# RWKV bonus sums formed once a head and spread later, and the sample values' products put ahead of the turned key tiles, in a one-layer HGRN2 + RWKV-7 + mixture-of-experts step

## Chip, cores, metric

One core of a Trainium2 chip. The metric is the device time of one execution in microseconds. TensorE is called PE here, VectorE DVE, ScalarE ACT, GpSimd POOL; SP is the engine that issues most of the DMAs.

## What is computed (the reference, cut)

A prompt of 256 rows and 64 sample rows (8 sequences of 8 tokens) of width 1024 go through one layer. After a norm and one input projection, half of the columns feed an HGRN2 group (4 heads of 128) and half an RWKV-7 group (8 heads of 64); their outputs are joined, projected and added; then comes a top-4-of-32 mixture of experts. The change touches only the RWKV group:

```python
k = k * (1.0 + (a - 1.0) * k_a)
S = S * w_t + sa * (kk_t * a_t) + v_t * k_t      # per token; y_t = S r_t
y = group_norm(y) * lnx_w + lnx_b
bonus = jnp.sum(r_h * k_h * r_k, axis=-1, keepdims=True) * v_h     # one sum a head and token
y = (y + bonus) * g
```

The experts' weights are 32 x (8 + 4) MiB, read once.

## The kernel before, in words

Everything is float32 and kept with features on the 128 partitions: an array such as `rbon`, `rr`, `rk`, `rv` holds four tiles j, each of 128 features (two heads of 64) by 320 tokens. The engines run one hand-written stream each, tied by semaphores. PE's stream sets the order of the first 300 us; its results go to eight PSUM banks by a table, `psum_units`: each unit (a stage with a number) is given a bank, `free(stage, i)` makes PE wait until the unit that held the bank before has been read (`<stage>_ready`), and `filled` counts `unit_filled` up, on which the readers wait (`wait_filled`).

In the order of PE's stream, around the change: `kss` and `kspread` (L1008, L1027; a sum over each head by 32 columns of the block matrix `blk`, and its spreading by a column of the identity, for the key norms), the HGRN outputs `ho` and `hosa` (up to L1086), the HGRN state product `hs2` (L1014) and projection 23, then the RWKV products `gM`, `gN`, `gT` (L1126, L1136), and a long solve. Behind it come:

- `Ys` (L1318 to L1320): the sample rows' values. For each j and each head p of the tile, three products of 64x64 add up in one quarter of bank 0. After each j stand four transposes of 128x128 (L1313), which turn a key tile (`btok`, `ktok`) to tokens.
- `UW` and `UX` (L1332), in two token tiles, then `bonus` (L1339): per j one product of the full `blk` with `rbon`, which gives each head's sum already on all of its 64 rows, in banks 4, 5, 0, 1.
- `C` (L1351), `S0` (L1505, L1508, in banks 3 and 4), `sendl`/`sendh` (L1490), `Q` (L1520), `Y0` (L1537, L1540).

ACT reads `btok`, `ktok`, `Ys`, `UW` and one `UX` out of PSUM (L2158 to L2165), DVE the other `UX` (L2775, L2776), with the decay of the sample states (`decayed`, L2771) before and after it, and then multiplies the four bonus banks by `rv` into `rbon` (L2781). POOL sends out the sample states of HGRN in eight DMAs (L837).

SP waits at L640 for these eight to have landed (`hgrn_out`) and for `Y0`, then reloads the input rows and begins the stream of the experts' weights, in pieces of 2 and then 4 MiB, into slots that it gets back from PE (`w_used`):

```python
sync.wait_ge(S("hgrn_out"), 16 * (NS + 1))
sync.wait_ge(S("unit_filled"), U("Y0", 2))
```

Of the kernel before, what the change touches and what calls it, by code (L numbers as in the profile page):

```python
# [81 lines left out]
def psum_units():  # L82

    u, turn, ends = [], [0], []

    def add(stage, n=1, at=None, ended=True):
        k = sum(1 for s, _, _ in u if s == stage)
        for i in range(n):
            if at is None:
                u.append((stage, k + i, turn[0] % 8))  # L90
                turn[0] += 1
            else:
                u.append((stage, k + i, at[i]))
            if ended:
                ends.append((stage, k + i))

    def end(stage, k):
        ends.append((stage, k))
    add("nmT", 1, (0,))
    add("hT", KT, (1, 2, 3, 4, 5, 6, 7, 0))  # L100
    add("proj", 1, (1,), ended=False)
    add("bc", 1, (2,))
    add("params", 1, (3,))
    end("proj", 0)
    turn[0] = 3
    add("proj", 12)
    turn[0] += 3
    for i, h in enumerate(LEVELS):
        if i % 2:
            add("proj", 2)  # L110
        if h < 64:
            add("lvl")
        else:
            add("cross")
        if h <= 4:
            add("seq")
    add("lvl")
    add("seq")
    add("proj")
    add("kstok", 3)  # L120
    for j in range(4):
        for stage, o in (("wpre", 0), ("apre", 4)):
            add(stage, 1, ((turn[0] + o + j) % 8,))
    add("gpre", 4)
    add("proj")
    t = turn[0]
    add("kss", 1, (t % 8,))
    add("hs1", 1, ((t + 4) % 8,))
    add("proj", 1, ((t + 5) % 8,), ended=False)
    add("kspread", 4, tuple((t + i) % 8 for i in range(4)))  # L130
    end("proj", 21)
    turn[0] = t + 6
    add("ho", 2)
    add("hosa", ended=False)
    add("proj")
    end("hosa", 0)
    add("hs2", 1, (1,))
    add("proj", 1, (7,))
    add("gM", 3, (2, 3, 1))
    add("gN", 3, (4, 5, 6))  # L140
    add("gT", 2, (7, 0))
    add("s0t", 4, (5, 6, 7, 0))
    add("gT", 1, (1,))
    add("Z", 3, (2, 3, 4))
    add("proj", 1, (5,))
    add("W", 3, (6, 7, 0))
    add("T", 3, (1, 2, 3))
    add("proj", 1, (4,), ended=False)
    add("Z", 3, (5, 6, 7))
    end("proj", 25)  # L150
    add("W", 3, (0, 1, 2))
    add("T", 3, (3, 4, 5))
    add("gK", 3, (6, 7, 0))
    add("proj", 1, (1,), ended=False)
    add("Z", 2, (2, 3))
    add("gRb", 3, (4, 5, 6))
    end("proj", 26)
    add("W", 2, (7, 0))
    add("T", 2, (1, 2))
    add("ht", 3, (4, 5, 6))  # L160
    add("proj", 1, (3,))
    add("vtok", 3, (4, 5, 6))
    add("Z", 2, (7, 0))
    add("Rs", 2, (1, 2), ended=False)
    add("proj", 1, (3,))
    add("W", 2, (4, 5))
    add("T", 2, (6, 7))
    end("Rs", 0)
    end("Rs", 1)
    add("hsend", 4, (0, 3, 4, 5))  # L170
    add("proj", 1, (6,))
    add("Z", 2, (4, 5))
    add("Us", 1, (1,))
    add("gRk", 3, (2, 3, 4))
    add("atok", 2, (5, 6))
    add("R0", 2, (7, 0))
    add("bks", 1, (1,))
    add("hsend", 4, (2, 3, 4, 5))
    add("W", 2, (6, 7))
    add("Ys", 1, (0,), ended=False)  # L180
    add("btok", 2, (1, 2))
    add("ktok", 2, (3, 4), ended=False)
    end("ktok", 0)
    end("Ys", 0)
    end("ktok", 1)
    for x in range(2):
        add("UW", 1, (6 + x,))
        add("UX", 1, (2 + x,))
    add("bonus", 4, (4, 5, 0, 1))
    add("C", 2, (6, 7))  # L190
    add("S0", 2, (3, 4), ended=False)
    add("sendl", 1, (2,))
    add("sendh", 1, (5,))
    end("S0", 0)
    end("S0", 1)
    add("Q", 2, (0, 1))
    add("sendl", 1, (2,))
    add("sendh", 1, (5,))
    add("Y0", 2, (6, 7))
    add("yc", 1, (2,))  # L200
    u.append(("xo", 1, 0))
    add("var", 1, (5,))
    add("yc", 1, (1,))
    u.append(("xo", 2, 3))
    add("var", 1, (4,))
    add("yc", 1, (6,))
    add("pst", 1, (5,))
    u.append(("xo", 0, 7))
    end("xo", 0)
    add("var", 1, (5,))  # L210
    end("xo", 1)
    end("xo", 2)
    add("h2T", 1, (4,))
    u.append(("xo", 3, 2))
    add("logit", 1, (5,))
    add("h2T", 2, (1, 6))
    u.append(("xo", 4, 7))
    add("fold", 1, (4,))
    add("logit", 1, (3,))
    add("fold", 1, (5,))  # L220
    end("xo", 3)
    add("h2T", 1, (1,))
    add("rank", 1, (0,))
    end("xo", 4)
    add("h2T", 1, (2,))
    add("logit", 1, (3,))
    add("fold", 1, (0,))
    add("rank", 1, (3,))
    add("bias", 1, (2,))
    assert len(ends) == len(u)  # L230
    return u, ends
# [82 lines left out]
def build(nc, A, O):  # L314
    ctx = ExitStack()
    with ctx:
# [539 lines left out]
        def _(pe):  # L856
            mm = nc.tensor.matmul

            def free(stage, i):

                n_ = UPOS[stage, i]
                if BEFORE[n_] is not None:
                    s, k, _ = UNITS[BEFORE[n_]]
                    s, k = {"nmT": ("params", 1), "bc": ("params", 2), "params": ("params", 3), "hT": (("hT", "hTo_lb")[k % 2], k // 2), "S0": ("S", k + 2), "Y0": ("Y", k), "xo": ("xo", k + 1)}.get(s, (s, k))
                    pe.wait_ge(S(f"{s}_ready"), k + 1)
                return banks[BANK[n_]]

# [215 lines left out]
            for y in range(2):  # L1083
                for p in range(2):
                    r = slice(64 * p, 64 * p + 64)
                    last = mm(b[r, P * y:P * y + P], ats[r, y, :], itoks[r, y, :], start=False, stop=True, skip_group_check=True)  # L1086
            filled(last, "hosa")
            hstate("hs2", 1)
            proj(23, 24)

# [18 lines left out]
            def half(x):  # L1109

                return slice(64 * x, 64 * x + 64)
# [202 lines left out]
                filled(last_, stage)  # L1314
            for j in range(4):
                for p in range(2):
                    o = b[half(p), half(j)]
                    mm(o, us[half(p), j, :], Rb_[2][half(p), j, :], start=True, stop=False, skip_group_check=True)  # L1318
                    mm(o, vtoks[half(p), j, :], Rk_[2][half(p), j, :], start=False, stop=False, skip_group_check=True)
                    last = mm(o, yts[half(p), j, :], ident[half(p), half(p)], start=False, stop=True, skip_group_check=True)  # L1320
                if j == 3:
                    filled(last, "Ys")
                turn_tokens(("btok", "ktok")[j // 2], (ra, rk)[j // 2], j % 2)
            pe.wait_ge(S("W_ready"), upto(4))
            pe.wait_ge(S("R0_ready"), 2)
# [1 line left out]
            for tile in range(2):  # L1327
                b = [free("UW", tile), free("UX", tile)]
                for j in range(4):
                    for a in range(2):  # L1330
                        for p in range(2):
                            last = mm(b[p][half(a ^ p), P * j:P * j + P], W_[p][half(a), 4 * tile + j, :], RA[half(a), p, tile, j, :],  # L1332
                                      start=True, stop=True)
                            if (j, a) == (3, 1):
                                filled(last, ("UW", "UX")[p])
            pe.wait_ge(S("rbon_in"), 4)
            for j in range(4):
                b = free("bonus", j)
                filled(mm(b[:, 0:NT], blk[:, :], rbon[:, j, :], start=True, stop=True), "bonus")  # L1339

            def head(x_, p_):
                return slice(P * (x_ % 4) + 64 * p_, P * (x_ % 4) + 64 * p_ + 64)
# [632 lines left out]
        def _(act):  # L1975
# [56 lines left out]
            for n, (j, _, _) in enumerate(PROJ):  # L2032
# [51 lines left out]
                if n == 21:  # L2084

                    act.wait_ge(S("cen_ready"), 1)
                    a(ec[:, :, :], cen[:, :, :], ACT.Exp, scale=-EDEC)
                    act.wait_ge(S("cen_ready"), 2)
                    act.wait_ge(S("unit_filled"), U("kss", 1))
                    a(tB[:, :, :], tA[:, :, :], ACT.Exp, scale=EDEC).then_inc(S("exp_ready"), 1)  # L2090
                    a(rs[:, :, :], rs[:, :, :], ACT.Exp, scale=-EDEC).then_inc(S("exp_ready"), 1)
                    act.wait_ge(S("exp_ready"), 1)
                    a(tA[:, :, :], tA[:, :, :], ACT.Exp, scale=-EDEC).then_inc(S("exp_ready"), 1)
                    for tile in range(2):
                        ready(cp(htok[:, 512 * tile:512 * tile + 512], wait_filled("ho", tile)[:, :]), "ho")
                    ready(cp(htok[:, 1024:W5], wait_filled("hosa", 0)[:, 0:256]), "hosa")
                    act.wait_ge(S("ho_ready"), 2)
                    act.wait_ge(S("hosa_ready"), 1)
                    act.wait_ge(S("ks_row_scale"), 1)
                    a(hsq, htok, ACT.Square).then_inc(S("osq"), 1)  # L2100
                if n == 23:
                    act.wait_ge(S("ks_row_scale"), 1)
                    for x in range(3):
# [295 lines left out]
        def _(dve):  # L2399
# [376 lines left out]
            signal(v.tensor_copy(o[64:128], b[0:64, :]), "UX_ready")  # L2776
            decayed(1)
            dve.wait_ge(S("gpre_ready"), 4)
            for j in range(4):
                b = wait_filled("bonus", j)  # L2780
                signal(v.tensor_tensor(rbon[:, j, :], rv[:, j, :], b[:, 0:NT], ALU.mult), "bonus_ready")  # L2781
# [141 lines left out]
            sent(0)  # L2923
            step_state(0)
            sent(1)
            dve.wait_ge(S("bonus_ready"), 4)
            for j in range(4):
                signal(v.scalar_tensor_tensor(out=rbon[:, j, :], in0=rbon[:, j, :], scalar=pcol("lnb", j), in1=rg[:, j, :],
                                              op0=ALU.add, op1=ALU.mult), "bg_ready")
# [226 lines left out]
```

## Time and profile before

| | |
|---|---|
| median of 3 runs | 1212.01 us (1211.21 to 1215.73) |
| the profiled execution | 1214.35 us, of which the span of the trace is 1212.4 us |
| PE busy | 1187.4 us (98%) |
| DVE, ACT, POOL busy | 440.9, 259.5, 44.7 us |
| read from HBM | 430.01 MB |
| granted PE clock | 0.998 of full speed over the span |

The profile is one execution. A row of the timeline has the start in us, the time from the first start to the last end, the engine, line, operation, operands and count, and in brackets the idle time ahead of it and what ended that. PE records each float32 matmul as two, so x8 are four matmuls; matmul rows overlap their neighbours, so what a group costs is read from start to start.

### The profile page before, as it was taken

What the parts mean: (1) busy time and instruction counts of PE and PEld (TensorE: products, weight loads), DVE (VectorE), ACT (ScalarE), POOL (GpSimd) and SP (SyncE); (2) the same over time, 40 slices, a digit from 0 to 9 for tenths busy, and PEclk for the clock granted to TensorE, in tenths of its full rate; (3) what the DMA queues carried; (4) which work ended last, traced back from release to release, by engine and by line L of the source; (5) the groups of instructions that cost most, each with busy time, mean ns of one, the idle gap of its engine ahead of it and who ended that gap; (6) DMA issues with size and microseconds to landing.
All of it is one profiled execution on the core that took longest, in us unless ns stands there. A gap on an engine that the chain in (4) does not pass through costs nothing.

```text
span 1212.4 us, 18239 instructions
## 1 busy us (share of the span) xinstructions
PE 1187.4 (98%) x7814; PEld 572.9 (47%) x7814; DVE 440.9 (36%) x962; ACT 259.5 (21%) x630; POOL 44.7 (4%) x101
## 2 busy tenths in 40 slices
PE   8999999999999999999999999999999999999996
PEld 6777677745344344444443444344444444343332
DVE  3357954753413332332233132313322323232324
ACT  3114435422221111111121212021111111111213
POOL 8000110100000000000000000000000000000000
PEclk9999999999999999999999999999999999999999
DMA  9732302498999999999999999999999999999996
GB/s 285 183 105 71 122 31 72 125 414 334 409 426 429 426 414 428 426 432 431 431 429 431 431 431 432 431 426 431 429 432 432 430 430 431 432 432 428 422 424 231
DMA packets 49387, 436.09 MB, mean 360 GB/s; under 512 B 11525, under 2 KB 26952, under 8 KB 31770
## 3 DMA queue, kind: packets, MB, share of 16 engines
q1 hardware_dynamic: 48180, 431.74, 86.4%
q0 software_dynamic: 960, 3.02, 0.8%
q8 instruction: 63, 1.03, 0.3%
q10 hardware_dynamic: 166, 0.15, 0.0%
q14 instruction: 18, 0.15, 0.0%
HBM read 430.01 MB, written 4.89 MB: 359 GB/s over the span
## 4 chain that ended last, share of the span: by engine, by line
PE 86%; DMA 10%; DVE 2%; issue 1%; SPq 0%; ACT 0%; DVEq 0%
PE bank L1634 33%; PE bank L1670 16%; PE bank L914 9%; PE bank L1600 7%; DMA ring<-in_w_gate_up 5%; PE bank L1704 4%; PE bank L1395 3%; DMA ring<-in_w_down 3%; PE bank L1661 3%; DMA mix<-in_w_gate_up 2%; PE bank L1695 1%; PE bank L1152 1%; PE bank L901 1%; PE bank L947 1%; DMA hx<-in_state_shift 0%
## 5 line engine op out<-in xcount | busy, mean ns | idle before, releaser
L1634 PE MATMUL bank<-ring,mix 128*64 128x512 f32 x1504 | 344.8, 598 | 3.3 <-DMA ring<-in_w_gate_up 3.1
L1634 PEld LDWEIGHTS bank<-ring,mix 128*64 128x64 f32 x1504 | 101.3, 136 | 201.0 <-issue 197.7
L1670 PE MATMUL bank<-ring,mix 128*64 128x512 f32 x736 | 168.2, 598 | 0.8 <-DMA ring<-in_w_down 0.8
L2986 DVE TENSOR_TENSOR hTb<-bank,w2a 128x512 f32<-128x512 f32 x32 | 22.1, 692 | 361.3 <-PE bank L1661 361.3
L914 PE MATMUL bank<-hTb,ring 128*128 128x328 f32 (+1 forms) x416 | 120.6, 444 | 0.0
L2218 ACT ACTIVATE mix<-bank,nf 128x256 f32<-128x256 f32 x64 | 26.8, 470 | 431.3 <-PE bank L1600 431.2
L1634 PE MATMUL bank<-mix 128*64 128x512 f32 x500 | 112.7, 595 | 1.8 <-DMA mix<-in_w_gate_up 1.8
L3046 DVE TENSOR_TENSOR mix<-mix,bank 128x512 f32<-128x512 f32 x70 | 48.2, 688 | 159.5 <-PE bank L1704 143.5
L914 PEld LDWEIGHTS bank<-hTb,ring 128*128 128x128 f32 x416 | 77.8, 192 | 33.8 <-issue 2.0
L1670 PEld LDWEIGHTS bank<-ring,mix 128*64 128x64 f32 x736 | 49.3, 136 | 89.9 <-issue 84.0
L1634 PEld LDWEIGHTS bank<-mix 128*64 128x64 f32 x500 | 35.1, 137 | 71.7 <-issue 70.0
L1600 PE MATMUL bank<-mix,hx 128*128 128x256 f32 x240 | 66.1, 418 | 0.0
L3014 DVE SCALAR_TENSOR_TENSOR y_low<-bank,gc,y_high 64x512 fp32r<-64x512 f32 x62 | 46.5, 750 | 49.6 <-ACT y_high L2293 49.1
L1600 PEld LDWEIGHTS bank<-mix,hx 128*128 128x128 f32 x240 | 55.5, 300 | 9.1 <-issue 8.4
L2293 ACT ACTIVATE y_high<-bank,gc 64x512 fp32r<-64x512 f32 x62 | 42.3, 682 | 74.1 <-DVE gc L3028 38.3
L2273 ACT COPY g2w<-bank 128x512 f32<-128x512 f32 x64 | 34.3, 593 | 99.8 <-PE bank L1634 99.8
L1670 PE MATMUL bank<-mix 128*64 128x512 f32 x240 | 54.8, 598 | 0.0
L1704 PEld LDWEIGHTS bank<-y_high,slot_rows 128*128 128x128 f32 (+1 forms) x96 | 16.2, 186 | 62.5 <-issue 62.5
L1661 PEld LDWEIGHTS bank<-idg,g2w 128*128 128x128 f32 x256 | 33.2, 209 | 26.0 <-issue 26.0
L2283 ACT ACTIVATE bank<-hTb 128x512 f32<-128x512 f32 x32 | 19.2, 602 | 113.9 <-DVE hTb L2988 113.9
L1704 PE MATMUL bank<-y_high,slot_rows 128*128 128x512 f32 (+1 forms) x96 | 42.3, 480 | 0.0
L1661 PE MATMUL bank<-idg,g2w 128*128 128x128 f32 x256 | 39.3, 296 | 0.0
(448 smaller groups left out, 1086.7 us busy)
## 6 DMA issues: line engine op xcount, KB each, us to landing
ring<-in_w_gate_up SPq DMA_DIRECT2D x30, 4096.0 KB, 22.9
ring<-in_w_gate_up SPq DMA_DIRECT2D x33, 2048.0 KB, 14.4
ring<-in_w_down SPq DMA_DIRECT2D x15, 4096.0 KB, 23.7
mix<-in_w_gate_up SPq DMA_DIRECT2D x10, 4096.0 KB, 23.7
ring<-in_w_down SPq DMA_DIRECT2D x14, 2048.0 KB, 13.8
mix<-in_w_gate_up SPq DMA_DIRECT2D x11, 2048.0 KB, 13.2
mix<-in_w_down SPq DMA_DIRECT2D x5, 4096.0 KB, 25.0
ring<-in_w_in SPq DMA_DIRECT2D x14, 1024.0 KB, 5.5
```

Source lines behind the costliest of these rows:

```text
L914: last_ = mm(b_[:, 0:nn], slot(chunk)[:, c, P * k:P * k + P], hT[:, c, 0:nn], start=(c == 0), stop=(c == KT - 1))
L1395: last_ = mm(o_, lhs_, wo[c_ // 4][:, c_ % 4, 512 * h_:512 * h_ + 512], start=(c_ == 0), stop=(c_ == KT - 1))
L1600: last_ = mm(o, rows_of(tile_, c, r), sel[tile_][0:TN[tile_], :], start=(first and tile_ == TORD[0]), stop=(tile_ == TORD[2]), skip_group_ ...
L1634: last_ = mm(b_[64 * half:64 * half + 64, :].rearrange("s (p q) -> s p q", q=4), toks, cols[:, half], start=(c == 0), stop=(c == KT - 1))
L1661: last_ = nc.tensor.transpose(b_[:, P * q:P * q + P], src[:, q:NCOL:4], ident[:, :])
L1670: last_ = mm(b_[r:r + 64, :], lhs, w[:, o:o + NCOL], start=(j == 0 and q == 0), stop=(j == 1 and q == 3))
L1704: last_ = mm(o[:, :], scatr[r[g], g, P * tile_:P * tile_ + P], y_[r[g], g, :], start=(y_ is yhir and g == half), stop=(stop and y_ is ylor ...
L2218: ins = a(xg[n // 4 % 2][:, 256 * c:256 * c + 256], b[:, 256 * x:256 * x + 256], ACT.Copy, scale=nf2[int(n // 4 >= EW // 4)][:, c:c + 1])
L2273: cp(o, b[:, :]).then_inc(S("gu_read"), 1)
L2293: ins = a(yhir[r, k, :], banks[2][r, :], ACT.Copy, scale=gc[r, g:g + 1])
L3014: ins = v.scalar_tensor_tensor(out=ylor[r, k, :], in0=banks[2][r, :], scalar=gc[r, g:g + 1], in1=yhif[r, k, :], op0=ALU.mult, op1=ALU.subt ...
L3046: ins = v.tensor_tensor(o, o, b[:, :], ALU.add)
```

## The change

A new unit `bsum` stands after `hosa`, in bank 0: four matmuls sum `rbon` over each head, every tile j into 32 rows of one bank, with every fourth column of `blk`. ACT copies that bank into `rbon[:, 0, :]`, after its square of the HGRN rows. Late in the stream `bonus` no longer multiplies with `blk`: per j, two matmuls that contract over 32 rows spread one row each over the 64 rows of a head. DVE now waits for all four bonus units before it overwrites `rbon`. And all of `Ys` runs first, with the two heads p side by side, before the 16 transposes.

```diff
@@ psum_units
     end("hosa", 0)
+    add("bsum", 1, (0,))
     add("hs2", 1, (1,))
...
-    add("Ys", 1, (0,), ended=False)
+    add("Ys", 1, (0,))
     add("btok", 2, (1, 2))
-    add("ktok", 2, (3, 4), ended=False)
-    end("ktok", 0)
-    end("Ys", 0)
-    end("ktok", 1)
+    add("ktok", 2, (3, 4))
@@ PE
             filled(last, "hosa")
+            pe.wait_ge(S("rbon_in"), 4)
+            b = free("bsum", 0)
+            for j in range(4):
+                last = mm(b[32 * j:32 * j + 32, 0:NT], blk[:, 0:P:4], rbon[:, j, :], start=True, stop=True)
+            filled(last, "bsum")
             hstate("hs2", 1)
@@ PE
             for j in range(4):
                 for p in range(2):
-                    o = b[half(p), half(j)]
-                    mm(o, us[half(p), j, :], Rb_[2][half(p), j, :], start=True, stop=False, skip_group_check=True)
-                    mm(o, vtoks[half(p), j, :], Rk_[2][half(p), j, :], start=False, stop=False, skip_group_check=True)
-                    last = mm(o, yts[half(p), j, :], ident[half(p), half(p)], start=False, stop=True, skip_group_check=True)
-                if j == 3:
-                    filled(last, "Ys")
+                    mm(b[half(p), half(j)], us[half(p), j, :], Rb_[2][half(p), j, :], start=True, stop=False, skip_group_check=True)
+                for p in range(2):
+                    mm(b[half(p), half(j)], vtoks[half(p), j, :], Rk_[2][half(p), j, :], start=False, stop=False, skip_group_check=True)
+                for p in range(2):
+                    last = mm(b[half(p), half(j)], yts[half(p), j, :], ident[half(p), half(p)], start=False, stop=True,
+                              skip_group_check=True)
+            filled(last, "Ys")
+            for j in range(4):
                 turn_tokens(("btok", "ktok")[j // 2], (ra, rk)[j // 2], j % 2)
@@ PE
-            pe.wait_ge(S("rbon_in"), 4)
+            pe.wait_ge(S("bonus_ready"), 1)
             for j in range(4):
+                r = slice(32 * j, 32 * j + 32)
                 b = free("bonus", j)
-                filled(mm(b[:, 0:NT], blk[:, :], rbon[:, j, :], start=True, stop=True), "bonus")
+                for p in range(2):
+                    c = 32 * j + 16 * p
+                    last = mm(b[half(p), 0:NT], ident[r, c:c + 1].broadcast_to([32, 64]), rbon[r, 0, :], start=True, stop=True)
+                filled(last, "bonus")
@@ ACT
                     a(hsq, htok, ACT.Square).then_inc(S("osq"), 1)
+                    ready(cp(rbon[:, 0, :], wait_filled("bsum", 0)[:, 0:NT]), "bonus")
@@ DVE
             dve.wait_ge(S("gpre_ready"), 4)
+            dve.wait_ge(S("unit_filled"), U("bonus", 4))
             for j in range(4):
                 b = wait_filled("bonus", j)
                 signal(v.tensor_tensor(rbon[:, j, :], rv[:, j, :], b[:, 0:NT], ALU.mult), "bonus_ready")
```

Line numbers after the change are some 2 to 11 higher than before. PE's stream between the last rows of the solve (L1152 before, L1155 after) and the transposes, before:

```order
L1152 MATMUL bank<-mix,hx 64x32 x31
L1318 MATMUL bank<-ring 64x64 [waits Us_ready,R0_ready,gRk_ready,gRb_ready]
L1319 MATMUL bank<-ring 64x64
L1320 MATMUL bank<-idg,lor 64x64
L1318 MATMUL bank<-ring 64x64
L1319 MATMUL bank<-ring 64x64
L1320 MATMUL bank<-idg,lor 64x64
L1313 MATMUL bank<-idg,mix 128x128 [waits bks_ready]
L1313 MATMUL bank<-idg,mix 128x128 x3
```

and the same place after, where L1320, L1322 and L1324 are the three products of `Ys` and L1316 the transposes:

```order
L1155 MATMUL bank<-mix,hx 64x32 x31
L1320 MATMUL bank<-ring 64x64 [waits Us_ready,R0_ready,gRk_ready,gRb_ready]
L1320 MATMUL bank<-ring 64x64
L1322 MATMUL bank<-ring 64x64 x2
L1324 MATMUL bank<-idg,lor 64x64 x2
L1320 MATMUL bank<-ring 64x64 x2
L1322 MATMUL bank<-ring 64x64 x2
L1324 MATMUL bank<-idg,lor 64x64 x2
```

The group of six stood four times with four transposes behind each; now the four groups follow each other, each product for both heads at once, and the 16 transposes come after them. The second place is PE's stream from `bonus` to the first products of `S0`, before:

```order
L1339 MATMUL bank<-mix,g2w 128x320 [waits ktok_ready,rbon_in]
L1339 MATMUL bank<-mix,g2w 128x320 [waits hsend_ready]
L1339 MATMUL bank<-mix,g2w 128x320 [waits Ys_ready]
L1339 MATMUL bank<-mix,g2w 128x320 [waits btok_ready]
L1351 MATMUL bank<-hTb,ring 64x64 [waits UX_ready,UW_ready,ktok_ready,btok_ready]
L1351 MATMUL bank<-hTb,ring 64x64 x31
L1505 MATMUL bank<-ring,hTb 64x64 [waits bonus_ready,UX_ready]
```

and after, where L1347 is `bonus`, L1360 `C` and L1514 the first product of `S0`:

```order
L1347 MATMUL bank<-mix,idg 64x320 [waits ktok_ready,bonus_ready]
L1347 MATMUL bank<-mix,idg 64x320
L1347 MATMUL bank<-mix,idg 64x320 [waits hsend_ready]
L1347 MATMUL bank<-mix,idg 64x320
L1347 MATMUL bank<-mix,idg 64x320 [waits Ys_ready]
L1347 MATMUL bank<-mix,idg 64x320
L1360 MATMUL bank<-hTb,ring 64x64 [waits UX_ready,UW_ready,ktok_ready,btok_ready]
L1360 MATMUL bank<-hTb,ring 64x64 x31
L1514 MATMUL bank<-ring,hTb 64x64 [waits bonus_ready,UX_ready]
```

Eight narrow matmuls stand for the four full ones, and the waits of what follows are the same.

## Rows read from the trace of the kernel before

**Rows 1.** Windows, whole kernel: stretch, length, busy of each engine, PEclk, DMA share, GB/s
```profile
600.00:800.00 200.00, 200.00 (x875) 83.43 (x876) 60.05 (x138) 33.06 (x86) 0.00 (x0) 1.00 1.00 430
```
**Rows 2.** Waits of SP's queue: who waited for whom, total, times, longest
```profile
SPq L640 <- PE bank L1540: 47.4, 1, 47.4
```
**Rows 3.** Timeline of SP's queue, start of the weight stream
```profile
236.57 0.49 SPq L587 DMA_DIRECT2D hx<-in_x_sample  x1
...
238.21 2.33 SPq L587 DMA_DIRECT2D ring<-in_w_gate_up  x5
```
**Rows 4.** Timeline of PE, 118 to 146 us, around the new unit's place
```profile
119.85 0.77 PE L1008 MATMUL bank<-hx,g2w 128*32 128x320 f32 x8
...
125.51 0.79 PE L1027 MATMUL bank<-mix,idg 32*64 32x320 f32 x16
...
136.82 0.65 PE L1086 MATMUL bank<-ring 64*64 64x128 f32 x8
...
142.91 1.16 PE L1126 MATMUL bank<-mix 64*64 64x64 f32 x64
145.75 0.62 PE L1136 MATMUL bank<-mix 64*64 64x64 f32 x13 [1.68 <-DVE ring L2624]
```
**Rows 5.** Timeline of ACT, same stretch
```profile
137.97 1.27 ACT L2100 ACTIVATE ring<-mix 128x1280 f32<-128x1280 f32 x1
139.15 0.41 ACT L2056 COPY raw<-bank 128x328 f32<-128x328 f32 x1
```
**Rows 6.** Timeline of DVE, same stretch
```profile
131.52 1.94 DVE L2603 SCALAR_TENSOR_TENSOR mix<-mix,par 128x320 f32<-128x320 f32 x4
...
140.97 0.48 DVE L2479 TENSOR_TENSOR hx<-raw 128x319 f32<-128x319 f32 x1
```
**Rows 7.** Chain that ended last, 207 to 226 us: start, us, what
```profile
207.96 0.41 PE bank L1283 x13
...
216.00 0.22 PE bank L1318 x2
...
216.63 0.59 PE bank L1313 x4
...
220.95 1.91 PE bank L1332 x64
222.86 2.35 PE bank L1339 x8
225.21 1.09 PE bank L1351 x64
```
**Rows 8.** Timeline of PE, 226 to 232 us
```profile
226.12 0.30 PE L1505 MATMUL bank<-ring,hTb 64*64 64x64 f32 x8
...
231.43 1.96 PE L1490 MATMUL bank<-ring,lor 32*64 32x256 f32 x32 [0.21 <-issue]
```
**Rows 9.** Timeline of ACT, 220 to 225 us
```profile
220.99 0.59 ACT L2158 COPY hTb<-bank 128x512 f32<-128x512 f32 x1 [0.66 <-PE bank L1313]
...
224.11 0.58 ACT L2165 COPY ring<-bank 64x512 f32<-64x512 f32 x1
```
**Rows 10.** Timeline of DVE, 220 to 241 us
```profile
220.47 1.28 DVE L2771 TENSOR_TENSOR mix<-mix,pc 128x512 f32<-128x512 f32 x2
222.15 0.69 DVE L2775 COPY ring<-bank 64x512 f32<-64x512 f32 x1 [0.40 <-PE bank L1332]
...
224.90 1.68 DVE L2781 TENSOR_TENSOR mix<-mix,bank 128x320 f32<-128x320 f32 x4
...
240.74 0.42 DVE L2791 TENSOR_TENSOR mix<-bank,dc 128x256 f32<-128x256 f32 x1 [4.58 <-PE bank L1364]
```
**Rows 11.** Line L837, POOL's eight DMAs: durations in ns, first and last start
```profile
L837 POOL DMA_DIRECT2D out<-ring x8: 750/751/763, 217.1 to 228.9; - x8
...
DMA to landing us min/median/max: 3.0/3.4/4.2
```
**Rows 12.** Waits of PE, 118 to 300 us: total, times, longest
```profile
PE bank L1152 <- issue: 1.8, 2, 1.4
```

More of the change, by code:

```diff
@@ L863, in free @@
                     s, k, _ = UNITS[BEFORE[n_]]
-                    s, k = {"nmT": ("params", 1), "bc": ("params", 2), "params": ("params", 3), "hT": (("hT", "hTo_lb")[k % 2], k // 2), "S0": ("S", k + 2), "Y0": ("Y", k), "xo": ("xo", k + 1)}.get(s, (s, k))
+                    s, k = {"nmT": ("params", 1), "bc": ("params", 2), "params": ("params", 3), "hT": (("hT", "hTo_lb")[k % 2], k // 2), "S0": ("S", k + 2), "Y0": ("Y", k), "xo": ("xo", k + 1), "bonus": ("bonus", k + 1), "bsum": ("bonus", 0)}.get(s, (s, k))
                     pe.wait_ge(S(f"{s}_ready"), k + 1)
@@ L2925, in _ @@
             sent(1)
-            dve.wait_ge(S("bonus_ready"), 4)
+            dve.wait_ge(S("bonus_ready"), 5)
             for j in range(4):
```

## The prediction

> **What bounds the kernel now.** I read the windows first. In the experts' part [rows 1] the DMA engines are busy all the time (share 1.00, 430 GB/s) while PE's records overlap without a gap. The weights are 32 x 12 MiB, 402.7 MB, and at 430 GB/s they take about 936 us of the 1212; nothing in the change touches that part. So the end of the kernel is the start of the weight stream, plus bytes over rate, plus what the slots hold it up on the way. The second view is SP's queue: it sat 47.4 us in one wait at L640, released by L1540, the last product of `Y0` [rows 2]; the input rows are issued at 236.57 and the first weights at 238.21 us [rows 3]. The wait before it, for POOL's eight DMAs, had ended by then: the last was issued at 228.9 us, is 0.75 us long and lands in 3.0 to 4.2 us [rows 11], so at 232.7 to 233.9 us, some 2.7 to 3.9 us before SP moved. What the change is worth is therefore how much earlier `Y0` is filled, one for one, up to 2.7 us and a little beyond. After `Y0` everything (output projection, router, first slots) hangs on the same chain and moves with it.
>
> **The early place: bsum.** It adds four matmuls of 128 rows by 32 columns over 320 tokens. That is the very shape of `kss`, whose eight records take 0.77 us [rows 4]. They stand behind `hosa`, which starts at 136.82 us and takes 0.65, so at about 137.5 us. Their input was ready at 131.52 + 1.94 = 133.46 us [rows 6]: no wait. All behind it on PE's queue (`hs2`, projection 23, `gM`) moves by 0.77: `gM` from 142.91 to 143.68. But the third part of `gM` waits 1.68 us for DVE's L2624 at 145.75 us [rows 4]. The cover is 1.68 us, the cost 0.77, so nothing is left to pay, as long as DVE is not made later itself. DVE would be, if ACT were late: ACT gets one more copy of 128x320 (0.41 us, the nearest copy) between the square that starts at 137.97 and the `raw` copy at 139.15 [rows 5]. `bsum` is full at about 138.3, before the square ends, so ACT does not wait; the raw copy ends at 139.56 + 0.41 = 139.97, and DVE reads it at 140.97 [rows 6]. 1.0 us of slack is left. If both covers were gone, this part would cost 0.77 or up to 1.2 us; the bound below nothing is excluded, since nothing is removed here. I take 0.
>
> **The late place on PE alone.** From the start of `Ys` to `UW` now: 220.95 - 216.00 = 4.95 us. It is four times 12 records of 64x64 in 216.63 - 216.00 = 0.63 us (52 ns each) and four transposes in 0.59 us [rows 7]. After it the products run as pairs of heads. The nearest row is L1283, 13 records in 0.41 us, 32 ns each: the same two quarters of the array, the same one bank [rows 7]. 48 x 0.032 = 1.54, and 4 x 0.59 = 2.36 for the transposes (an upper bound, they now follow each other): 3.90, so 1.05 us less. `bonus` is now 2.35 us [rows 7]; its new form is that of `kspread`, 16 records in 0.79 us [rows 4]: 1.56 less. Together PE could be 2.6 us earlier at `C`, at 225.21 - 2.6 = 222.6 us.
>
> A rule speaks against the first of these. The Trainium skill, TensorEngine Tiling (Array Packing), Restrictions and Gotchas (Gotcha 1: PSUM Pressure), says that different row tiles cannot access the same PSUM bank at once. By it the heads' pairs would not overlap in bank 0, and `Ys` would stay at 52 ns a record. By this rule, the row of L1283 does not agree, since its two row halves write one bank at 32 ns a record.
>
> **What C waits for then.** `C` needs both `UX` and both `UW`. With PE alone, the second `UX` is full at 216.00 + 3.90 + 1.91 = 221.8 us. ACT then has three copies of 0.58 us with 0.02 between (`UW` and the two halves of `UX`, the last of which now starts at 224.11) [rows 9], so it is done at 223.6. It comes that far in time: of the key copies the last, which now starts at 220.99 behind a wait for L1313 [rows 9], starts about 1 us earlier too. DVE copies the first `UX`: it waits only 0.40 us for it now, behind a `decayed` of 1.28 us that starts at 220.47 and is not held by PE [rows 10]. So DVE gains 0.40 us and no more: copies at 221.75 instead of 222.15, done at 223.1. `C` starts at 223.6 (now 225.21) and ends, 1.09 later [rows 7], at 224.7.
>
> **What S0 waits for: the term that decides.** `S0` takes bank 4, which held bonus unit 0, so PE waits until DVE has multiplied that unit into `rbon`. Now DVE's four multiplications start at 224.90 and take 1.68 us [rows 10]; the first is done at about 225.38 (0.48 us for a first 128x320 on DVE, as the row of L2479 [rows 6]), and PE comes at 226.12 [rows 8], 0.74 us later: hidden. After the change DVE starts 0.40 earlier, at 224.50 (the new wait for all four bonus units ended at about 222.6 on PE), and unit 0 is free at 224.98. PE has been ready since 224.7, and starts `S0` at 225.02. That is 226.12 - 225.02 = 1.10 us earlier. PE then comes out of an idle instead of a full pipeline; today the first record of `S0`, at 226.12, overlaps the end of `C` at 225.21 + 1.09 = 226.30 [rows 7, 8] by 0.18, and that overlap is lost in part. I take off 0.1. Gain: 1.0 us of the 2.6.
>
> Behind it nothing takes more. `sendh` and `Q` need bonus units 1 to 3, freed at 0.40 us steps. The 0.21 us idle at 231.43 [rows 8] is, I think, DVE's sum out of the first `send` products, which follows PE and moves with it. Further on DVE waits 4.58 us for PE at 240.74 [rows 10], so it has room.
>
> **Sum.** 0 (early place) - 1.0 (late place) = -1.0 us. Against the profiled execution: 1214.35 - 1.0 = 1213.35, span 1211.4. That execution lies 2.3 us above the median of the runs, so the forecast for the median is 1212.01 - 1.0 = 1211.0 us.
>
> **Rivals.**
> - *All of PE's gain arrives* (-2.6 us, 1209.4): if DVE's work before the bonus is shorter than I read. For it: PE's saving is solid. Against: DVE's stretch from 220.47 to 226.6 has one gap, of 0.40 us [rows 10]. 0.10.
> - *The pairs in one bank do not overlap.* `Ys` stays at 4 x 0.63 + 2.36 = 4.9 us; only `bonus` gains. The second `UX` is full at 222.8, ACT done at 224.7, `C` ends at 225.8, 0.46 us earlier than now, and `S0` with it: -0.5 us with a little less idle, 1211.5. For it: the single records of L1318. Against: L1283. This is what the skill's page would make of it. 0.10.
> - *Nothing arrives* (1212.0): the gain is eaten between `Y0` and the slots, where the stream waits for several steps of the router. 0.20.
> - *Slower.* PE stands still for up to 1.4 us at places where nothing is waited for (L1152, issue 1.8 us in two stops [rows 12]). The change puts 8 records more ahead of the solve and 8 more into `bonus`. If that brings one more such stop, or makes one longer, in the stretch from 147 to 216 us where PE never waits for another engine, it is paid in full: +1.4 - 1.0 = +0.4, 1212.4, and with a second, 1213.8. It decides from 1.0 us of added standstill on. For it: the stops are there. Against: few records are added. 0.15.
> - *The forecast*, -0.7 to -1.3: 0.45.
>
> **Range and chances.** The cases reach from 1209.4 to 1213.8. A median of a few runs moves by itself: three runs before lay between 1211.21 and 1215.73. Leaving out the outer tenths I say 1208.9 to 1213.8; the likeliest case alone 1210.4 to 1211.9. No change under 0.5% (6 us) can be told by a measurement of this kernel from none, and all cases lie within 3 us: within 0.5% 0.95, faster 0.02, slower 0.03 (a bound on the weight stream that I do not see).
>
> **What would show it.** Right: `kss`'s 0.77 us again at the new line before `hs2`, and PE's wait for L2624 cut from 1.68 to about 1.0; `Ys` and the transposes in 3.9 us or a little less; `bonus` in 0.8; PE idle for about 1 us before `C`, released by ACT's last `UX` copy, and 0.3 us before `S0`, released by DVE's first multiplication; first weights at about 237.2 us. Wrong: no idle before `S0` (then DVE was earlier), 12 records of `Ys` in 0.6 us (no overlap), SP released by POOL's DMAs instead of PE, or an end that does not follow the start of the weights.

## The result and the profile after

| | before | after |
|---|---|---|
| median of runs, us | 1212.49 (22 runs, 1210.91 to 1215.73) | 1215.73 (22 runs, 1212.91 to 1217.45) |
| ratio to before | | 1.0024, 95% interval 1.0018 to 1.0031 |
| profiled execution, time / span, us | 1214.35 / 1212.4 | 1214.93 / 1213.2 |
| instructions | 18239 | 18274 |
| PE records | | 7830, busy 1185.3 us |

The change costs 0.24%, about 2.9 us (the two medians, which the ratio does not go by, lie 3.2 apart), where a gain of 1.0 us was forecast. The time lies above the range. The loss is under the 0.5% taken as the bound of what can be told, but 22 runs a side tell it from nothing.

The weight stream is as before [rows 1], by the windows of the same stretch (all engines, PEclk, DMA share, GB/s):

```profile
600.00:800.00 200.00, 200.00 (x877) 83.59 (x877) 59.74 (x138) 33.05 (x86) 0.00 (x0) 1.00 1.00 430
```

The start of the stream is still PE's to decide, and it did not come earlier by 1 us net. These rows of after are from the waits and the timeline of SP's queue, and answer to [rows 2, 3]; the last one is the first group of transfers in the stream proper:

```profile
SPq L638 <- PE bank L1549: 46.4, 1, 46.4
...
236.07 0.49 SPq L585 DMA_DIRECT2D hx<-in_x_sample  x1
...
237.71 2.37 SPq L585 DMA_DIRECT2D ring<-in_w_gate_up  x5
...
297.30 7.57 SPq L585 DMA_DIRECT2D ring<-in_w_gate_up  x4
```

That last group starts at 297.01 us in the trace of before. From it to the end of the span are 1212.4 - 297.01 = 915.4 us before and 1213.2 - 297.30 = 915.9 after, and between 914.6 and 915.9 in every kernel below. So what is won or lost lies ahead of it.

**The two places that the change edits** went as forecast in this trace. PE's timeline of after (start, us, what, idle before and its releaser), to be held against [rows 4, 7, 8]:

```profile
135.65 0.77 PE L1089 MATMUL bank<-mix,g2w 128*32 128x320 f32 x8
...
144.00 0.62 PE L1139 MATMUL bank<-mix 64*64 64x64 f32 x13 [0.98 <-DVE ring L2634]
...
216.33 0.33 PE L1320 MATMUL bank<-ring 64*64 64x64 f32 x4
216.46 0.31 PE L1322 MATMUL bank<-ring 64*64 64x64 f32 x4
216.58 0.31 PE L1324 MATMUL bank<-idg,lor 64*64 64x64 f32 x4
...
217.87 1.96 PE L1316 MATMUL bank<-idg,mix 128*128 128x128 f32 x16
219.79 1.98 PE L1337 MATMUL bank<-ring,hx 64*64 64x128 f32 x64
221.69 0.79 PE L1347 MATMUL bank<-mix,idg 32*64 32x320 f32 x16
223.95 1.16 PE L1360 MATMUL bank<-hTb,ring 64*64 64x64 f32 x64 [1.46 <-ACT ring L2175]
225.53 0.34 PE L1514 MATMUL bank<-ring,hTb 64*64 64x64 f32 x8 [0.42 <-DVE mix L2792]
```

`bsum` takes 0.77 us and the wait for DVE behind it fell from 1.68 to 0.98. `Ys` and its transposes take 219.79 - 216.33 = 3.46 us in place of 4.95, `bonus` 0.79 in place of 2.35. PE then waits where it was forecast to wait, for ACT's last `UX` copy and for DVE's first bonus multiplication, whose rows in the timelines of ACT and DVE are:

```profile
223.01 0.58 ACT L2175 COPY ring<-bank 64x512 f32<-64x512 f32 x1
```
```profile
222.14 0.69 DVE L2785 COPY ring<-bank 64x512 f32<-64x512 f32 x1
...
224.89 1.68 DVE L2792 TENSOR_TENSOR mix<-mix,bank 128x320 f32<-128x320 f32 x4
```

From the first record of `Ys` to the first of `S0` are 225.53 - 216.33 = 9.20 us. Before, the first single record of `Ys` stood at 215.93, and `S0` at 226.12: 10.19. The gain of the late place is 0.99 us in this trace, and it was a good one for it: the stretch is 10.2 us in all four traces of kernels with neither part, but 9.82 in a second trace of this same program (experiment 4) and 9.48 and 9.59 in the two variants of it in experiments 7 and 9. In the second trace DVE's first `decayed`, which does not hang on PE, stands 5.11 us behind the start of `Ys` and not 4.49, and `S0` is as much later. So the gain is 0.4 to 1.0 us, by how DVE stands; with the `Ys` part alone it is 0.3 to 0.5 (9.88 and 9.68), with the bonus part alone 0.1 (10.08, twice).

**Where the time went**: the stops of PE for which the profile names nothing ("issue"), ahead of both `Ys` and the stream. PE's timeline of after, these stops alone (one of 0.29 us at 230.89, of another kind, is left out):

```profile
151.27 1.66 PE L1155 MATMUL bank<-hx,mix 64*64 64x64 f32 x64 [1.46 <-issue]
...
162.83 0.30 PE L1163 MATMUL bank<-hx,mix 64*64 64x32 f32 x2 [0.85 <-issue]
...
172.74 0.31 PE L1163 MATMUL bank<-hx,mix 64*64 64x32 f32 x5 [0.49 <-issue]
...
201.34 0.46 PE L1275 MATMUL bank<-ring 64*32 64x64 f32 x32 [1.32 <-issue]
...
216.05 0.43 PE L1155 MATMUL bank<-mix,hx 64*64 64x32 f32 x14 [0.48 <-issue]
...
233.79 0.28 PE L1549 MATMUL bank<-ring 64*64 64x64 f32 x3 [0.35 <-issue]
...
237.53 0.50 PE L1385 MATMUL bank<-mix 64*64 64x64 f32 x9 [0.53 <-issue]
```

and of before (likewise without one of 0.21 us at 231.43):

```profile
153.10 0.99 PE L1152 MATMUL bank<-hx,mix 64*64 64x64 f32 x53 [1.40 <-issue]
...
172.39 1.09 PE L1126 MATMUL bank<-mix 64*64 64x64 f32 x59 [0.85 <-issue]
...
200.90 0.42 PE L1272 MATMUL bank<-ring 64*32 64x64 f32 x23 [1.12 <-issue]
...
215.69 0.31 PE L1152 MATMUL bank<-mix,hx 64*64 64x32 f32 x5 [0.37 <-issue]
...
234.53 0.28 PE L1540 MATMUL bank<-ring 64*64 64x64 f32 x3 [0.30 <-issue]
```

Before had no stop near 162 and none after `Y0` (the last of its rows lies in `Y0`). A stop can fall inside a group of equal records and cut it: in before, 8 of a group's 64 records stand ahead of the stop near 150 and 56 behind it, the 53 of the row and 3 more; in after all 64 stand behind. The stop comes 8 records earlier in the code, as many as `bsum` added. Between the first four stops of before its windows count PE's records (length, PE busy, records, PEclk, DMA share, GB/s):

```profile
151.75:171.60 19.85, 18.43 (x507) 1.00 0.10 40
171.60:199.85 28.25, 27.39 (x760) 1.00 0.22 78
199.85:215.40 15.55, 14.33 (x378) 1.00 0.01 3
```

507, 760 and 378 are about 4, 6 and 3 times 126.6: the stops stand at a fixed distance in the program, not where some work is done. Each record has a weight load beside it and there are some waits for semaphores between them, so 126.6 records are about 256 instructions. Counted with these, before's five stops fall on PE's instructions 2497, 3521, 5058, 5826 and 6850, those of after on 2498, 3010, 3521, 5057, 5825, 6849 and 7106. All of them are 193 or 194 above a multiple of 256. So is every "issue" stop of 0.30 us or more from 147 to 241 us in the fourteen traces, but for one at 195; the short ones (0.15 to 0.29 us) at L1490 or its counterpart are not, and are of another kind. The Trainium skill, Runtime: NRT & Kernel Launch, Instruction fetch mechanics, says that an engine's code comes in blocks of 256 instructions, and that crossing into one is mostly hidden. The distance agrees. "Mostly hidden" agrees by count and not by price: of the 20 such places from 147 to 241 us before shows a stop at five, and these cost 0.30 to 1.40 us. That what PE stops for is its code is thus a reading of these distances; no view shows the fetch itself.

Why the stop near 162 is new can be read off the same count. Instruction 3009 of before lies among the wide matmuls of a projection (128x328, eight records in 2.47 us from 162.08 on), and nothing stops there. With 16 instructions more ahead it lies two records (the x2 in the row of after) before that projection, among products of 64x32.

In the trace of after the stop near 150 is followed by a stretch at a granted clock of 0.50, the 1.2 GHz level. PE's windows of after, then of the change's bonus part alone (below), which had a longer stop and kept its clock:

```profile
150.00:152.00 2.00, 0.73 (x40) 0.93 1.03 418
152.00:154.00 2.00, 2.00 (x53) 0.50 0.33 125
154.00:156.00 2.00, 2.00 (x6) 0.72 0.01 2
```
```profile
152.00:154.00 2.00, 0.09 (x4) 1.00 1.01 410
154.00:156.00 2.00, 2.00 (x82) 1.00 0.24 88
```

The same two in PE's timeline, at the stop's end and at the next group of that line:

```profile
151.27 1.66 PE L1155 MATMUL bank<-hx,mix 64*64 64x64 f32 x64 [1.46 <-issue]
...
159.00 1.14 PE L1155 MATMUL bank<-mix,hx 64*64 64x32 f32 x64
```
```profile
153.91 1.16 PE L1158 MATMUL bank<-hx,mix 64*64 64x64 f32 x64 [2.28 <-issue]
...
160.07 1.14 PE L1158 MATMUL bank<-mix,hx 64*64 64x32 f32 x64
```

**One sum over the traces.** Each from one execution, us: from the release of `gM`'s third part (the row with the wait for L2634, or its counterpart) to SP's input rows; PE's "issue" stops in that stretch; from the input rows to the stream's group above; and the stop behind `Y0`, which lies there. Kernels that the next section introduces are in the table too.

| kernel | to input rows | stops in it | on to the stream | stop behind `Y0` |
|---|---|---|---|---|
| before (1214.35) | 90.8 | 4.25 | 60.4 | none |
| before, again (1212.43) | 89.0 | 3.08 | 60.4 | none |
| `Ys` part alone (1210.35) | 89.0 | 3.28 | 60.4 | none |
| bonus part alone (1214.39) | 90.9 | 5.04 | 60.6 | none |
| before + 4 idle matmuls (1215.30) | 90.6 | 4.23 | 61.2 | 0.66 |
| after (1214.93) | 92.1 | 5.24, and half clock | 61.2 | 0.53 |
| after, again (1215.94) | 92.2 | 5.40, and half clock | 61.8 | 1.08 |

The first trace of before is of an execution 1.9 us above its median, with stops to match; the second (experiment 3), at 1212.43, is the typical one. Against it after has 2.2 us more of stops up to the input rows, about 1.6 us for the half clock (for the same records 159.00 - 151.27 = 7.73 us against 160.07 - 153.91 = 6.16 in the bonus part alone, at full clock), and 1.0 less for the late place: +2.8 of the +3.1 us in the table. The stop behind `Y0` adds 0.8. That is 3.9 us in a pair of traces whose times differ by 2.5: the third part of `gM` is released at 145.76 in before and at 144.00 in after, with nothing edited that would make it earlier by that much. The repeat of after closes too: 2.3 of stops, 1.2 of half clock and 0.4 less for the late place are 3.1 of its +3.2. The idle matmuls' trace does not: the stops are 1.15 of its +1.68.

**The new stops over all traces.** Stops, us, at the two places that before does not have:

| kernels | near 162 | behind `Y0` |
|---|---|---|
| without added instructions (before twice, `Ys` part, and experiments 6, 8 and 11) | none in six traces | none in six |
| 16 more ahead of the solve (after twice, bonus part, idle matmuls, and experiments 7, 10 and 12) | 0.30 to 1.00 in all seven | 0.53 to 1.08 in six of seven |
| 256 more (experiment 9) | none | 0.77 |

### The profile page after: what moved, and what is told of

Same layout as the page of the kernel before. It is cut to its first block, busy times and chain, and to the rows that moved or that the text cites. A ratio compares the mean times of both kernels' runs of the same rounds, so it can differ in the third digit from the quotient of the medians.

```text
span 1213.2 us, 18274 instructions
## 1 busy us (share of the span) xinstructions
PE 1185.3 (98%) x7830; PEld 571.9 (47%) x7830; DVE 441.0 (36%) x962; ACT 259.6 (21%) x631; POOL 43.8 (4%) x101
## 4 chain that ended last, share of the span: by engine, by line
PE 86%; DMA 10%; DVE 3%; issue 1%; ACT 0%; SPq 0%; DVEq 0%
PE bank L1643 33%; PE bank L1679 16%; PE bank L912 9%; PE bank L1609 7%; DMA ring<-in_w_gate_up 5%; PE bank L1713 4%; PE bank L1404 3%; DMA ring<-in_w_down 3%; PE bank L1670 3%; DMA mix<-in_w_gate_up 2%; PE bank L1704 1%; PE bank L899 1%; PE bank L1155 1%; PE bank L945 1%; PE bank L1746 0%
```

## Experiments

Every ratio is to the kernel before on the same chip, with its 95% interval; in brackets this median and that of before, us. Theory A: the 8 records of `bsum` shift PE's later code against the places where PE stops for code. B: the new order of `Ys` costs. C: the waits and copies that `bsum` brings cost. D: the stop near 150 us is PE's next code queued behind the 2 MiB load of `w_out`.

**1 and 2. The change in two halves.** One kernel takes the order of `Ys` alone, one takes `bsum` and `bonus` alone.

```diff
 # ys_only
-    add("Ys", 1, (0,), ended=False)
+    add("Ys", 1, (0,))
...
 # bonus_only
+    add("bsum", 1, (0,))
...
```

> Before, with only the new order of Ys and the transposes. Theory A (the place of PE's instructions in the blocks in which its code comes decides how long PE stands still for nothing it waits for): Ys shortens to about 3.7 us from 4.95, no record is added, so the stops stay where they were; the gain reaches S0 in part, -0.3 to -0.5 us, 1212.0. Theory B (the new order itself costs, for instance by what its earlier or later copies do to the engines behind): this kernel is slower than before by 1 to 3 us.

Measured: 1.0001 (0.9992 to 1.0010) [1212.02, 1212.45].

> Before, with only the sums formed once a head and spread later (Ys as before). Theory A: 8 PE records more ahead of the solve move all later code by that much against its blocks, the stops at 162 and 172 us appear here as in the changed kernel, and most of the +2.9 us is here: +2 to +3. Theory B (the loss is in the order of Ys): this kernel is at 1212 +- 0.5.

Measured: 1.0030 (1.0019 to 1.0041) [1215.00, 1212.45]. The bonus part holds the whole loss; B falls. A and C both stand, since this half has both the records and the waits.

**3 and 4. An attempt to pad PE's code.** `pe.nop()` 32 and 224 times at the head of PE's program, before any matmul.

```diff
+            for _ in range(32):
+                pe.nop()
```

> Before, with 32 empty instructions at the head of PE's stream, where PE waits for the first input anyway. No operation of the kernel moves against another. Theory A: the stops of PE shift and grow as in the changed kernel, the time rises by 1 to 3 us. Theory C (the loss comes from waits or copies that the change adds): no difference to before, within 0.5 us.

> The changed kernel with 224 empty instructions at the head of PE's stream, which with the 32 added ones make 256. Theory A: the stops come back to where they were before the change (171.5, 199.8 us), and the time falls below before by the forecast 1 us: about 1211.5, some 3 to 4 under the changed kernel. Theory C: it stays at the changed kernel's time, 1215.7.

The built programs have no such instruction, so both are repeats. Before: 1.0004 (0.9995 to 1.0013) [1212.26, 1212.45]; after: 1.0013 (1.0004 to 1.0023) [1214.14, 1212.45]. They say nothing on A, but how far one and the same program moves between batches of runs: 0.0011 for after, 1.3 us. Its trace has the stops and the half clock again.

**5. Real padding of before.** Four matmuls of one column at PE's head, into a bank that nobody reads; the outputs are unchanged. They run while PE waits for its first rows, until 4.06 us, and end before.

```diff
+            for _ in range(4):
+                mm(bank("nmT", 0)[0:32, 0:1], ident[:, 0:32], ident[:, 0:1], start=True, stop=True)
```

> Before, with 4 matmuls of one column at the head of PE's stream, whose results nothing reads, where PE waits for the first input anyway (8 records more, as many as bsum adds; the empty instructions of the runs before do not show in the built program, so those two were repeats of before and of the changed kernel). Theory A (the place of PE's code against its blocks): the stops at 151.7, 171.5 and 199.8 us come 8 records earlier and one near 162 us appears, as in the changed kernel; +1.5 to +3 us, 1214 to 1215.5. Theory C (the loss comes from what bsum does where it stands): no difference, within 0.5 us.

Measured: 1.0023 (1.0009 to 1.0036) [1214.49, 1212.14]. No wait, no copy and no order differs from before, and the loss is of the size of the change's. Its "issue" stops in PE's timeline:

```profile
152.63 1.10 PE L1154 MATMUL bank<-hx,mix 64*64 64x64 f32 x60 [1.19 <-issue]
...
162.52 0.24 PE L1162 MATMUL bank<-hx,mix 64*64 64x32 f32 x1 [0.74 <-issue]
...
172.30 0.30 PE L1162 MATMUL bank<-hx,mix 64*64 64x32 f32 x4 [0.40 <-issue]
...
238.01 1.96 PE L1397 MATMUL bank<-ring,mix 128*128 128x512 f32 x4 [0.66 <-issue]
```

The new stop at 162 and the new one behind `Y0` are there, in a kernel that differs from before by 16 instructions of PE. This is A, and C is not needed: the place of the code alone makes a loss of this size, +2.8 us with an interval of 1.1 to 4.4. How it divides the traces leave open, since the stops up to the input rows (4.23 us) are 1.15 more than in the typical trace of before, but no more than in the other.

**6 to 8, 10. The `w_out` load out of the way**, in this order in before, in the changed kernel, in the `Ys` part and in the bonus part. Behind the 15th projection chunk SP issues 2 MiB of `w_out` (at 142.37 us in after), and the DMA engines are busy with share 1.0 until about 152.7. Here it goes out behind chunk 13, 15 to 17 us earlier.

```diff
+                if n == 13:
+                    load(wo[1], w_out[:, 4:8, :], "x1_wo1_in")
...
-            load(wo[1], w_out[:, 4:8, :], "x1_wo1_in")
```

> Before, with the 2 MiB load of the second half of w_out issued behind the 14th projection chunk (about 126 us) instead of behind the 15th (143.4 us), when PE is in wide matmuls. Theory D (PE's stop at 151 us is its next code waiting behind this load): the stop of 1.40 us goes or falls under 0.5, and the time falls by about 1 us, 1211.3. If D is wrong: stop and time unchanged.

> The changed kernel with the same earlier load. Theory D: the stop of 1.5 to 2.3 us at 150 us goes and with it the half clock behind it; 2 to 2.5 us under the changed kernel, 1213. The stop at 162 us stays if it has another cause. If D is wrong: 1215 and the stop as it was.

> Before, with the new order of Ys alone (run before at 1212.0, the same as before) and the earlier load. Theory D: 1 to 1.5 us under before, 1211, the best version so far. If the gain of Ys is still eaten between Y0 and the stream: as the one with the earlier load alone.

> The fourth corner of the square: only the sums once a head, with the earlier load of w_out. If the parts add up, it stands to the earlier load alone as the changed kernel with the earlier load does to Ys with it (+1.1 us): 1213.3. If the late place's gain is real once the stops are small: 1212 or under.

| | load as it was | load early |
|---|---|---|
| neither part | 1.0004 (the repeat) | 1.0002 (0.9991 to 1.0013) |
| `Ys` part | 1.0001 | 0.9988 (0.9978 to 0.9997) |
| bonus part | 1.0030 | 1.0009 (1.0000 to 1.0018) |
| both (the change) | 1.0024, repeat 1.0013 | 1.0004 (0.9995 to 1.0013) |

In all four traces the stop near 150 is gone (and in the two of experiments 11 and 12, which have the early load too), and in that of the whole change the clock is 1.00 there. PE's windows and stops of the changed kernel with the early load:

```profile
150.00:152.00 2.00, 2.00 (x71) 1.00 0.01 4
```
```profile
160.84 0.30 PE L1164 MATMUL bank<-hx,mix 64*64 64x32 f32 x2 [0.44 <-issue]
...
199.29 0.46 PE L1276 MATMUL bank<-ring 64*32 64x64 f32 x32 [1.32 <-issue]
```

D holds for that stop in so far as the stop is there only when the load is in flight, and for it alone: those at 161 and 199 stay, and the one behind `Y0` (0.53). That PE's code stands in a queue behind the load is one way to read it; that PE's fetch is only slowed while the DMA engines are full is another, and no run tells them apart. Nor is the half clock gone for good. The traces of the `Ys` part and of the bonus part with the early load, and that of experiment 12, have such a stretch behind their stop near 199 (1.39, 1.60 and 1.32 us); here is PE in the first of them:

```profile
198.00:200.00 2.00, 2.00 (x32) 0.69 0.03 8
200.00:202.00 2.00, 2.00 (x4) 0.50 0.00 0
```

The bonus part gets back 0.0021, the whole change 0.0009 to 0.0020 by which of its two batches one takes. The two columns are from different batches, and experiment 4 moved by 0.0011 for that reason alone. Before gets back nothing that can be measured, though a stop of 1.40 us is gone from its trace; its interval reaches from -1.1 to +1.6 us, so a gain of 1.0 us would fit in it and the stop's full 1.4 does not.

**9. A whole block more.** 60 of the one-column matmuls at the head of the changed kernel, 240 instructions; with the 16 of `bsum` that makes 256.

> The changed kernel with 60 one-column matmuls at the head of PE's stream, whose results nothing reads (120 records; with the 8 of bsum about the distance between two stops). Theory A: behind bsum the stops come back to where they stood before the change (8 records into the first product of the solve, 1.40; near 171.5; near 199.8), and the one at 162 is gone; from L1139's release to the start of the weight stream it takes 1.5 to 2.5 us less than the changed kernel did. The head may cost up to 1.5 us itself, so the time is 1212 to 1214. Theory C (bsum's own waits and copies): no stop moves, the time rises by what the head costs.

Measured: 1.0038 (1.0025 to 1.0051) [1216.79, 1212.76]. The head was not free: its row lasts 6.56 us from 1.86 on and delays PE past the arrival of its first rows at 4.06, and all behind starts later (the third part of `gM` at 148.22, against 145.75 in before and 144.00 in after). Its time can't be used. Its stops can:

```profile
155.71 0.99 PE L1157 MATMUL bank<-hx,mix 64*64 64x64 f32 x53 [1.53 <-issue]
...
174.46 1.09 PE L1131 MATMUL bank<-mix 64*64 64x64 f32 x59 [0.32 <-issue]
...
202.97 0.42 PE L1277 MATMUL bank<-ring 64*32 64x64 f32 x23 [1.12 <-issue]
```

They cut the groups where before's did (x53, x59 as above; x23 in its row at 200.90), and the stop at 162 is gone. The place of a stop goes by PE's instruction count modulo 256. From the release of `gM`'s third part to the input rows are 89.3 us here, 92.1 in after. The stop behind `Y0` did not go:

```profile
239.47 0.21 PE L1387 MATMUL bank<-mix 64*64 64x64 f32 x1 [0.77 <-issue]
```

The 8 records that `bonus` itself has more still shift the code behind it by 16 instructions, so the 256 undo the early place's shift and not this one.

**11 and 12. The order on DVE.** With the early load, DVE first does both `UX` copies and the bonus multiplications, and the two `decayed` after them.

```diff
-            decayed(0)
...
-            decayed(1)
...
+            decayed(0)
+            decayed(1)
```

> Ys alone with the earlier load, and DVE's stream reordered: the copies of UX and the bonus multiplications first, the decay of the sample states (two times 1.28 us) behind them. If S0 waits for DVE's first bonus multiplication, as the trace says (0.47 us), this wait goes and the time falls by up to 0.5 us, to 1210.8. If not: the same as without it.

> The changed kernel with the earlier load and the same reordering on DVE. The waits of 1.69 us before C and 0.47 before S0 both hang on DVE's two decays; with them behind, ACT's copy of the second UX is the bound (C about 0.3 us earlier) and S0 follows without a wait: -0.5 to -1 us against the same without the reordering, 1211.5.

Measured: the `Ys` part 0.9981 (0.9972 to 0.9989) [1210.27, 1212.76], the whole change 0.9990 (0.9981 to 0.9999) [1211.66, 1212.76]. PE's timeline of the first:

```profile
221.13 1.16 PE L1351 MATMUL bank<-hTb,ring 64*64 64x64 f32 x64
222.11 0.30 PE L1505 MATMUL bank<-ring,hTb 64*64 64x64 f32 x8
```

`S0` no longer waits for DVE (0.42 us in after, 0.47 in the `Ys` part), and neither does it in the trace of the second. The `Ys` part with both other edits is the best kernel found, 2.5 us under before by medians. Against the same kernel without the order on DVE the gain is 0.0007, with overlapping intervals; for the whole change it is 0.0014, with intervals that just overlap. Neither is shown.

## Why the prediction was wrong

**Right.** The stream sets the end and moves with `Y0`. The cover of `bsum` (wait 1.68 to 0.98, forecast 1.0). The pairs of heads in one bank overlap: 12 records of `Ys` in 216.69 - 216.33 = 0.36 us, 30 ns each, against 32 forecast, so the rule of the Trainium skill, TensorEngine Tiling (Array Packing), Gotcha 1: PSUM Pressure, does not hold here either. The transposes, taken at their old spacing as an upper bound, were 0.4 us shorter than that. The waits at `C` (forecast from ACT, 1 us or so; 1.46) and `S0` (from DVE, 0.3; 0.42). The late place: 1.0 forecast, 0.99 in the trace of after. That they meet so closely is luck: 0.4 to 0.7 in the other traces with both parts, since DVE's own start, which the forecast took from one trace, moves by 0.6. What each half of it gains (0.3 to 0.5 and 0.1 in the traces) is too little to be seen in runs of one half.

**The step that failed** is the early place: "The cover is 1.68 us, the cost 0.77, so nothing is left to pay", and "I take 0". It priced the time of `bsum`'s eight records where they stand, and not that they are 16 instructions ahead of all of PE's later code. Four idle matmuls at the head, without any wait, cost 0.0023. That is +2.8 us (1.1 to 4.4), where the prediction had 0; the change's net loss is 2.9, and with the gain of the late place added, 3.3 to 3.9 had to be found.

**The rival "Slower"** had the mechanism (a stop more or a longer one, paid in full from 147 to 216 us), at a chance of 0.15 and +1.4 us a stop. The rows it named [rows 12] were the sign. It was mis-sized twice: one shift moves all stops at once, and one of the new ones lies behind `Y0`, where no term looked. Up to the input rows the stops grew by 2.2 us (against the typical trace of before) and the clock took about 1.6; the stop behind `Y0` added 0.8: 4.6 us by this pair of traces. "Few records are added" was no argument against it, since it is not their number but the place that counts. The other rivals (1209.4, 1211.5, 1212.0) are out, though "Nothing arrives" named the stretch from `Y0` to the slots, in which the 0.8 was lost. Misleading, too, was the chance of 0.95 for within 0.5% as a guide: it was true of the size, and it hid a loss that 22 runs resolve.

**Open.** Why a stop is 0.4 us at one place and 1.3 at another when the DMA engines have little to do (share 0.03 from 160 to 165 us in after). Why the clock fell after a stop of 1.46 us in after and not after one of 2.28 in the bonus part alone; it fell in five of the fourteen traces within 150 to 204 us, behind stops of 1.32 to 2.28 us, and stayed at full speed behind others as long. So the half clock's share of the loss is not separated by an experiment. The runs of after give a hint: the 11 with a mean clock of 0.998 or 0.999 have a median of 1214.6 us, the 11 with 0.995 to 0.997 one of 1217.0, so some 2 us of the loss are there without it; the repeat of after does not show this split (1214.0 and 1214.1). Why before gains nothing measurable from the early load. Each of these would want several traces of one program, as single ones scatter by 2 us.

## What to carry to other kernels

Where PE runs thousands of small matmuls and waits for nobody, list its "issue" stops with the count of records between them. Any edit that adds or removes PE instructions ahead of such a stretch shifts them all, so that a few microseconds of a measured difference may have nothing to do with the edit; pad the old kernel with the same number of idle instructions and time that too. And look at what bulk load is in flight at a stop: issued earlier, it can take the stop away.

## What the runs showed of the hardware

- PE stops of up to 2.3 us stand at places 256 instructions apart (about 126.6 matmul records with their weight loads), in dense runs of small matmuls and at some of these places only: 5 of 20 in before. 256 more instructions bring them back to the same records.
- The stop that meets the 2 MiB load (DMA share 1.0, 418 GB/s) was 1.19 to 2.28 us long in eight traces, and in the six with the load issued 15 to 17 us earlier there was none.
- The granted clock was 0.50 for a while behind five of the stops of 1.32 to 2.28 us, and 1.00 behind others of 1.32 to 2.28. With the same records it cost 1.2 and 1.6 us where it could be compared.
- Matmuls of 64x64 in two row halves that write one bank ran at 30 ns a record, with two heads by turns; 52 ns when each head's three followed one another [rows 7].
